# The opening of a two-block transformer kernel by half sections, and log counts added to the scores by TensorE

## The chip, the core and the metric

The kernel runs on one core of a Trainium2 chip. A core has TensorE (PE in the profile; PEld is its loading of weights), VectorE (DVE), ScalarE (ACT), GpSimd (POOL) and SyncE (SP), which here issues the loads. Each engine executes its own instructions in the order in which the program holds them; between engines there are only semaphores. The metric is the device time of one execution in microseconds (us), lower is better.

## The reference

Two blocks of two layers each, on 256 positions of width 1024, all in float32. What the change touches is the first block, in whose two layers `l` one finds:

```
mod = silu(c) @ w_mod[l] + b_mod[l]              # 1024 x 6144, one row
sh1, sc1, gt1, sh2, sc2, gt2 = split(mod, 6)
h = rms_norm(x, g) * (1 + sc1) + sh1
q_d, k_d, v_d, cq, ckv, k_rope = split(h @ w_in[l], ...)   # 1024 x 1952
# dilated heads (8 heads of 64), mixture of three window/dilation pairs
s = q.k * 64**-0.5 - slope_h * |distance|
...
# latent heads (8 heads): q = rms_norm(cq) @ w_q_up, its last 32 columns per head
# are normed and rotated: [x1*cos - x2*sin, x2*cos + x1*sin]
```

The mixture of the three dilated branches equals one softmax over all pairs of query and key whose scores have the logarithm of a count added: how many of the three branches see that pair. These log counts, 128 partitions x 512 for both tiles of queries, are a constant of the kernel and the same for all heads. Then follow the output product, an MLP, and the second block (stick-breaking and forgetting attention, a dense MLP and 8 experts), which the change does not touch.

## The kernel before

**Weights.** The kernel reads about 380 MB, nearly all of it float32 weights. SP loads them in pieces of 1 MB into a ring of six buffers, `raw`. A product in near float32 precision takes three passes of a rounded type (fp32r): ScalarE copies a piece rounded (`split`, L665, tile `w_high`), VectorE subtracts to get the remainder (`rest`, L1270, tile `w_low`), and TensorE multiplies high by high, high by low and low by high (`passes`, L2194). Activations are split in the same way (`h_high`, `h_low`). PE, ACT and DVE each hold such steps in an order that was written out by hand; `rest_to(w)` and `split_to(w)` mean all pieces up to `w`.

**Modulation.** Each section (l, s) of `mod` is computed from four pieces of `w_mod`, its quarters. The ones of the opening are (0,0) and (0,1), shift and scale of the first norm, and (0,2), the first gate. There a quarter is 256 columns by all 1024 rows: PE multiplies by a copy of silu(c) scaled by 1/32 (`c32`, in the profile c_columns_shared) into four strips of a bank (L2308, 16 matmuls), ACT copies the strips out (`store_rows`), PE adds them over the partitions with four tiny matmuls (`reduce_mod`, L2327), and DVE's `store_first(q)` adds the bias, 2 of the 8 blocks of 128 features at a time. Later sections are made in other ways, among them `BY_ROWS`: a quarter is 256 rows by all columns, 16 matmuls of 128x256 with 32 equal columns (L2301), read back by one transpose of 32x32 squares (L1407) and an add (L1409).

**The opening.** The first norm goes by blocks: DVE scales a block (`scaled_block`, L1351), ACT adds the shift and rounds (`h_high`, L756), DVE makes the remainder (`low_part`, L1340). It is done in four pairs, one per quarter, with the eight products of quarters between them. The pieces of `w_in` come in the order: columns from 1536 rows 0 to 511 (w0), the same columns rows 512 to 1023 (w1), then columns 0 to 511 (w2, w3) and 512 to 1023 (w4, w5) in two halves each. PE's `first_chunk` multiplies w0 against blocks 0 to 3, `second_chunk` w1 against blocks 4 to 7. Where PE has nothing to do, `turn_idly` (L2380) and `keep_busy` (L2268) issue matmuls whose results nobody reads. After w1 PE turns a stage of small vectors, which DVE's `store_vectors` (L1456, L1457) copies; then come w2, the positions (L2422 to L2424), w3, and the quarters of (0,2), their last two in front of the query up-projection (q_up).

**Latent and dilated stage.** When all of `w_in` is multiplied, PE does q_up (w6), kv_up (w7) and the rest of the w_in pieces (w8, w9), then the dilated heads, two at a time: `score_pair` (L2497, 8 matmuls), DVE's `max_head` (L1622) adds a bias to the scores and takes the maximum, ACT makes the exponentials, PE turns them (L2253) and multiplies by the values (L2539). The bias of a head is made by GpSimd: L628 scales the distances, L629 adds the log counts, into one of two tiles (dilated_bias, turned) that alternate, and a tile is free again when DVE has read it. DVE also rotates the latent queries between the heads (`mla_rotated`, L1605, and `mla_joined`, L1609 and L1610), and `mla_keys` (L1601) scales the latent keys. PE's `turn_mla` (L2564) needs both. In the first layer PE reduces section (0,2) (L2327, 16 matmuls) after the first `score_pair`, and DVE stores it (`store_mod(0, 2)`, L1409) after the first pair of maxima.

## Time and profile before

| | us |
|---|---|
| median of 3 runs | 1695.75 |
| lowest and highest | 1695.21, 1695.86 |
| the profiled execution, whole | 1694.58 |
| its span, first to last instruction | 1692.8 |
| its mean granted TensorE clock | 0.999 |
| PE busy in the span | 1656.1 |

A timeline row gives the start in us from the start of the span, the duration, engine, line and operation, out<-in by the program's names, and the shapes; "x16" says that 16 instructions stand in that row as one group, and the duration is then that of the group. In brackets stands the idle time of the engine just before, with what ended it. Matmuls are pipelined: the next one starts before the row of the last one ends, so the pace is read from the distance of two starts. Rows of the chain of waits follow the work back from the last instruction of the kernel, so they say whose lateness would move the end.

### The profile page before, as it was taken

To read this page: it belongs to the slowest core of one execution; us is meant where nothing else is said; L and a number is where in the kernel's file an instruction comes from. 1 tells how busy PE (TensorE), PEld (TensorE's weight loads), DVE (VectorE), ACT (ScalarE), POOL (GpSimd) and SP (SyncE) were. 2 spreads that over 40 slices of the span, in tenths; PEclk is the share of its full clock that TensorE was granted. 3 is DMA by queue.
4 is the path that set the end of the run, shared out by engine and by line. 5 is a ranking of instruction groups with operands and counts; after the bars stand their busy time and mean duration, and the time that the engine had idled before them with its cause. 6 is when DMAs were issued, how large, how long until landed. Compare 5 with 4: busy or idle time off the path is not lost.

```text
span 1692.8 us, 26664 instructions
## 1 busy us (share of the span) xinstructions
PE 1656.1 (98%) x10402; PEld 1422.0 (84%) x10402; DVE 1198.4 (71%) x1491; ACT 963.5 (57%) x1274; POOL 88.6 (5%) x105
## 2 busy tenths in 40 slices
PE   7999999999999999999999999999999999999998
PEld 5767898887688998898999999899888787887876
DVE  3775887777678555657585545557589888999887
ACT  4675534456754444546564434546567777667765
POOL 2050000003300000000000000000000000000000
PEclk9999999999999999999999999999999999999999
DMA  9765788845368655643256555553356999999995
GB/s 342 279 208 173 271 278 283 278 138 176 119 235 288 198 186 187 196 150 125 100 177 212 185 184 187 178 172 101 121 191 225 351 331 332 345 320 344 341 336 179
DMA packets 266362, 381.64 MB, mean 225 GB/s; under 512 B 8299, under 2 KB 201121, under 8 KB 266258
## 3 DMA queue, kind: packets, MB, share of 16 engines
q1 hardware_dynamic: 264592, 377.26, 66.8%
q0 software_dynamic: 1104, 1.76, 0.3%
q8 instruction: 72, 1.18, 0.3%
q10 hardware_dynamic: 562, 1.18, 0.2%
q14 instruction: 32, 0.26, 0.0%
HBM read 379.12 MB, written 1.05 MB: 225 GB/s over the span
## 4 chain that ended last, share of the span: by engine, by line
PE 83%; DVE 8%; ACT 4%; POOL 2%; issue 2%; DMA 1%; ACTq 0%; DVEq 0%
PE bank L2194 71%; DVE w_low L1270 4%; PE bank L2253 3%; ACT w_high L665 3%; PE bank L2509 1%; PE bank L2751 1%; DMA raw<-in_w_mod_dram 1%; PE bank L2539 1%; DVE mod_sums L1388 1%; PE bank L2301 1%; DMA x<-in_x_dram 1%; DVE turned L1351 1%; POOL dilated_bias L628 1%; POOL dilated_bias L629 1%; PE bank L2744 1%
## 5 line engine op out<-in xcount | busy, mean ns | idle before, releaser
L1270 DVE TENSOR_TENSOR w_low<-raw,w_high 128x2048 fp32r<-128x2048 f32 (+2 forms) x315 | 690.0, 2194 | 226.5 <-ACT w_high L665 225.0
L665 ACT ACTIVATE w_high<-raw 128x2048 fp32r<-128x2048 f32 (+3 forms) x333 | 596.4, 1797 | 219.3 <-PE bank L2194 211.0
L2194 PE MATMUL bank<-h_high,w_high 128*128 128x256 f32 x1200 | 342.8, 286 | 0.2
L2194 PE MATMUL bank<-h_high,w_low 128*128 128x256 f32 x1200 | 339.8, 283 | 0.0
L2194 PE MATMUL bank<-h_low,w_high 128*128 128x256 f32 x1200 | 339.8, 283 | 0.0
L2194 PE MATMUL bank<-w_high,h_high 128*128 128x512 f32 (+2 forms) x768 | 301.0, 392 | 8.5 <-DVE w_low L1270 7.5
L2194 PE MATMUL bank<-w_high,h_low 128*128 128x512 f32 (+2 forms) x768 | 292.1, 380 | 0.0
L2194 PE MATMUL bank<-w_low,h_high 128*128 128x512 f32 (+2 forms) x768 | 291.7, 380 | 0.0
L2194 PEld LDWEIGHTS bank<-h_high,w_high 128*128 128x128 f32 x1200 | 230.1, 192 | 5.3 <-issue 3.4
L2194 PEld LDWEIGHTS bank<-h_low,w_high 128*128 128x128 f32 x1200 | 230.1, 192 | 1.2
L2194 PEld LDWEIGHTS bank<-h_high,w_low 128*128 128x128 f32 x1200 | 230.0, 192 | 0.0
L2194 PE MATMUL bank<-w_high,act_high 128*128 128x512 f32 x544 | 213.7, 393 | 1.5 <-DVE act_low L1718 0.8
L2194 PE MATMUL bank<-w_low,act_high 128*128 128x512 f32 x544 | 211.7, 389 | 0.0
L2194 PE MATMUL bank<-w_high,act_low 128*128 128x512 f32 x544 | 211.3, 388 | 0.0
L2194 PEld LDWEIGHTS bank<-w_high,h_high 128*128 128x128 f32 x768 | 144.4, 188 | 45.0 <-DVE w_low L1270 14.2
L2194 PEld LDWEIGHTS bank<-w_high,h_low 128*128 128x128 f32 x768 | 144.4, 188 | 27.3
L2194 PEld LDWEIGHTS bank<-w_low,h_high 128*128 128x128 f32 x768 | 144.8, 189 | 24.1
L2194 PEld LDWEIGHTS bank<-w_high,act_high 128*128 128x128 f32 x544 | 102.3, 188 | 23.3 <-issue 1.3
L2194 PEld LDWEIGHTS bank<-w_high,act_low 128*128 128x128 f32 x544 | 102.1, 188 | 21.6
L2194 PEld LDWEIGHTS bank<-w_low,act_high 128*128 128x128 f32 x544 | 102.4, 188 | 18.8
L947 ACT ACTIVATE turned<-bank 128x512 f32<-128x512 f32 x32 | 19.1, 597 | 111.2 <-PE bank L2194 111.2
L1388 DVE SCALAR_TENSOR_TENSOR mod_sums<-raw,c_columns,mod_sums 128x512 f32<-128x512 f32 x70 | 52.6, 751 | 2.1
(355 smaller groups left out, 1822.4 us busy)
## 6 DMA issues: line engine op xcount, KB each, us to landing
raw<-in_w_gu_exp_dram SPq DMA_DIRECT2D x160, 512.0 KB, 5.4
raw<-in_w_in_dram SPq DMA_DIRECT2D x52, 1024.0 KB, 5.3
raw<-in_w_mod_dram SPq DMA_DIRECT2D x48, 1024.0 KB, 5.9
raw<-in_w_dn_exp_dram SPq DMA_DIRECT2D x40, 1024.0 KB, 6.4
raw<-in_w_mlp_in_dram SPq DMA_DIRECT2D x32, 1024.0 KB, 5.9
raw<-in_w_mlp_out_dram SPq DMA_DIRECT2D x32, 1024.0 KB, 5.2
raw<-in_w_gu_dense_dram SPq DMA_DIRECT2D x22, 1024.0 KB, 5.1
raw<-in_w_out_dram SPq DMA_DIRECT2D x16, 1024.0 KB, 5.1
```

The costliest lines, as they stand in the source:

```text
L628: step(nc.gpsimd.tensor_scalar(dst[:, :], dist[:, :], -(2.0 ** -(h + 1)), None, ALU.mult))
L629: nc.gpsimd.tensor_tensor(dst[:, :], dst[:, :], con[:, C_LNM:C_LNM + TT * S], ALU.add).then_inc(bias_ready, 1)
L665: return nc.scalar.activation(dst, src, ACT.Copy, scale=scale)
L947: nc.scalar.activation(relu[:, 0, slot, :], psum[slot][:, :], ACT.Relu).then_inc(f_one[l], 1)
L1270: V.tensor_tensor(wlo[w % SPLIT][:, 0:n], raw[raw_of(w) % RAW][:, 0:n], whi[w % SPLIT][:, 0:n].bitcast(F32), ALU.subtract).then_inc(raw_us ...
L1351: V.scalar_tensor_tensor(f, turned_bank(n, k), scale(k), rs_row, ALU.mult, ALU.mult).then_inc(h_float, 1)
L1388: ins = V.scalar_tensor_tensor(acc, vk, ccol[:, k:k + 1], acc, ALU.mult, ALU.add)
L2194: ins = T.matmul(out, lhsT, rhs, start=start and i == 0, stop=stop and i == len(pairs) - 1)
L2253: return T.transpose(out, src, ident)
L2301: ins = T.matmul(mod_strips_of(l, s)[32 * g:32 * g + 32, :], ccol[:, 2 * q + k:2 * q + k + 1].to_broadcast([P, 32]), rows[:, g, :, :], sta ...
L2509: ins = T.matmul(psum[e][:, S * t:S * t + S], qT[:, m, P * t:P * t + P], kT[:, m, :], start=True, stop=True)
L2539: ins = T.matmul(psum[4][DH * e:DH * e + DH, 0:S], v, pturn[:, e, S * kt:S * kt + S], start=kt == 0, stop=kt == TT - 1, skip_group_check=True)
```

## The change

It has three parts.

**Opening.** A quarter of (0,0) and (0,1) is now 512 columns by 512 rows, and its 16 matmuls are 128x128 with the unscaled `ccol`. They go straight into strips in bank 6 (first half of the features) or bank 0 (second half), so ACT's `store_rows` and PE's `reduce_mod` are gone for these sections; `store_first(half)` waits for four products, transposes, adds and scales for both sections, and is followed by four blocks of the norm instead of two. (0,2) becomes a section by rows: it has no `store_rows` or reduction either, `store_mod(0, 2)` moves from after the first maxima to ahead of `rest_to(w + 6)`, and PE waits for it ahead of q_up instead of ahead of the value product. The pieces of `w_in` come in another order, in both layers: w0 (columns from 1536) and w1 (columns 0 to 511) with rows 0 to 511, then w2 and w3 the same with rows 512 to 1023. PE multiplies all of w0 and w1 between the first half's products and the second half's, where blocks 4 to 7 were made beside w0 before.

**Log counts.** GpSimd splits the log counts once per layer (three instructions), PE adds them to the scores by eight more matmuls per pair of heads, and GpSimd's L629 is gone for all heads.

**Queries.** The six instructions of the rotation go from DVE to GpSimd, between the biases of heads 3 and 4; `mla_keys` moves ahead by a pair, and DVE waits for the rotation ahead of `store_mod(l, 3)`.

```diff
-    after = {(0, 0): [-1, -1, 0, 1], (0, 1): [-1, -1, 0, 1], (0, 2): [2, 3, 4, 5]}
+    after = {(0, 0): [-1, -1, 1, 1], (0, 1): [-1, -1, 1, 2], (0, 2): [3, 4, 5, 5]}
...
-BY_ROWS = ((0, 3), (0, 4), (1, 3), (1, 4))
+BY_ROWS = ((0, 2), (0, 3), (0, 4), (1, 3), (1, 4))
...
         def first_norm():
...
+            def high(blocks):
+                high_blocks(0, blocks, lambda k: modc[:, 0, k:k + 1])
             norm_squares(0)
-            store_rows(0, 1, 0)
-            store_rows(0, 0, 1)
             store_rs(0)
...
+            high(range(2))
             split_to(0)
...
+            high(range(2, 4))
+            split_to(2)
+            high(range(4, KD))
...
+        def store_first(half):
+
+            dve.wait_ge(mod_product, 4 * half + 4)
+            c = slice(4 * half, 4 * half + 4)
+            step(V.transpose(mod_turned, first_strips(half)))
+            columns = mod_turned.rearrange("p (s k i) -> p s k i", s=2, i=32)[:, :, :, 0]
+            biases = vec[:, V_BM:V_BM + 16].rearrange("p (s k) -> p s k", s=2)
+            step(V.tensor_tensor(modc[:, 0:2, c], columns, biases[:, :, c], ALU.add))
+            step(V.scalar_tensor_tensor(modc[:, 1, c], modc[:, 1, c], 1.0, vec[:, V_G1 + 4 * half:V_G1 + 4 * half + 4], ALU.add, ALU.mult))
+            V.sem_inc(mod_stored, 1)
...
+            for half in range(2):
+                store_first(half)
+                if half == 0:
                     dve.wait_ge(rs_out, 1)
+                for k in range(4 * half, 4 * half + 4):
                     scaled_block(0, k, scale_of)
+                    if k % 4:
+                        low_part(0, k - 1, shift_of)
+                low_part(0, 4 * half + 3, shift_of)
+                if half == 0:
+                    rest_to(2)
...
             if l == 0:
                 store_vectors()
-            rest_to(w + 3)
+            rest_to(w + 4)
...
             V.tensor_tensor(latlo, latent, lathi.bitcast(F32), ALU.subtract).then_inc(lat_low, 1)
+            if l == 0:
+                store_mod(0, 2)
             rest_to(w + 6)
...
+        multiply_first(0, 1)
         spread_rs(0)
...
+        turn_idly(2)
+        multiply_first(1, 0)
+        turn_idly(2)
+        multiply_first(1, 1)
+        turn_idly(2)
+        keep_busy(4, 5, 0)
...
+        natural(0, 0, W0, [psum[4 + t] for t in range(TT)], True, False, 0)
+        multiply_first(0, 2)
+        natural(1, 0, 512, [psum[6 + t] for t in range(TT)], True, False, None, [0])
+        multiply_first(0, 3)
+        natural(1, 0, 512, [psum[6 + t] for t in range(TT)], True, False, None, [1])
+        multiply_first(1, 2)
+        turn_idly(4, 1)
+        multiply_first(1, 3)
+        turn_idly(4, 1)
+        later_chunk(4, W0, 2)
...
+            if l == 0:
+                pe.wait_ge(mod_stored, stored_of(0, 2))
             pe.wait_ge(proj_out, 4 * l + 2)
...
+                pe.wait_ge(counts_ready, l + 1)
+                for e in range(2):
+                    for t in range(TT):
+                        for i, counts in enumerate((counts_high, counts_low)):
+                            ins = T.matmul(psum[e][:, S * t:S * t + S], ident_high, counts[:, S * t:S * t + S],
+                                           start=False, stop=i == 1, skip_group_check=True)
+                    ins.then_inc(head_scored, 1)
...
-                step(nc.gpsimd.tensor_scalar(dst[:, :], dist[:, :], -(2.0 ** -(h + 1)), None, ALU.mult))
-                nc.gpsimd.tensor_tensor(dst[:, :], dst[:, :], con[:, C_LNM:C_LNM + TT * S], ALU.add).then_inc(bias_ready, 1)
+                nc.gpsimd.tensor_scalar(dst[:, :], dist[:, :], -(2.0 ** -(h + 1)), None, ALU.mult).then_inc(bias_ready, 1)
```

What stands in a row on TensorE around the last two quarters of the opening. Before (banks 4 and 5 take the columns from 1536, 128x416 an instruction; L2308 is a quarter, L2327 its reduction, L2268 idle matmuls):

```order
L2194 MATMUL bank5<-w_high,h_low 128x416
L2327 MATMUL bank7<-ones,mod_sums 128x1 x2
L2308 MATMUL bank6<-raw2,c_columns_shared 32x256 x8
L2268 MATMUL bank1<-w_high 128x512 x2
L2327 MATMUL bank7<-ones,mod_sums 128x1 x2
L2268 MATMUL bank1<-w_high 128x512 x3
L2308 MATMUL bank0<-raw3,c_columns_shared 32x256 x8
L2194 MATMUL bank4<-w_high,h_high 128x416
```

The last quarter (bank 0) came after w0, the 24 matmuls of 128x416 into banks 4 and 5. Now, from the end of w1 on, which fills banks 6 and 7 (L2276 is a quarter, L2331 idle matmuls, L2162 the passes):

```order
L2162 MATMUL bank7<-w_high,h_high 128x512
L2162 MATMUL bank7<-w_low,h_high 128x512
L2162 MATMUL bank7<-w_high,h_low 128x512
L2276 MATMUL bank0<-raw2,c_columns 32x128 x16
L2331 MATMUL bank1<-x,constants 128x256 x4
L2276 MATMUL bank0<-raw4,c_columns 32x128 x16
L2331 MATMUL bank1<-x,constants 128x256 x4
L2162 MATMUL bank4<-w_high,h_high 128x416
```

The last quarter of the opening (from buffer 4) now stands behind 24 matmuls of 128x416 and 24 of 128x512.

On VectorE, behind the last remainder of the first norm, before (L1270 is `rest`, L1456 and L1457 `store_vectors`):

```order
L1340 SCALAR_TENSOR_TENSOR h_low<-turned,mod_columns,h_high 128x256 [waits h_high_ready] x2
L1270 TENSOR_TENSOR w_low<-raw,w_high 128x2048 [waits weights_high_done]
L1456 COPY vector_columns<-bank 128x128 [waits setup_tensor]
L1457 CAST rope_products<-dilated_bias 1x256
L1270 TENSOR_TENSOR w_low<-raw,w_high 128x2048 [waits weights_high_done,setup_vector]
```

And now (L1324 is the remainder of a block, L1437 and L1438 `store_vectors`, L1254 `rest`):

```order
L1324 SCALAR_TENSOR_TENSOR h_low<-turned,mod_columns,h_high 128x256 [waits h_high_ready] x2
L1437 COPY vector_columns<-bank 128x128 [waits setup_tensor]
L1438 CAST rope_products<-dilated_bias 1x256
L1254 TENSOR_TENSOR w_low<-raw,w_high 128x2048 [waits weights_high_done,setup_vector]
L1254 TENSOR_TENSOR w_low<-raw,w_high 128x2048 [waits weights_high_done]
```

The wait for the turned stage now stands ahead of both `rest` steps, those of w3 and w4. Further on in the same engine, ahead of q_up's piece, before:

```order
L1558 TENSOR_TENSOR act_low<-turned,act_high 128x768 [waits latent_high]
L1270 TENSOR_TENSOR w_low<-raw,w_high 128x1536 [waits weights_high_done]
L1307 TENSOR_TENSOR statistics<-statistics 128x16 [waits rsqrt_guess_ready]
```

And now, with `store_mod(0, 2)` (L1388, L1390) between:

```order
L1539 TENSOR_TENSOR act_low<-turned,act_high 128x768 [waits latent_high]
L1388 STREAM_TRANSPOSE rope_products<-bank 128x256 [waits mod_quarter_multiplied]
L1390 TENSOR_TENSOR mod_columns<-rope_products,vector_columns 128x8 [waits vector_step]
L1254 TENSOR_TENSOR w_low<-raw,w_high 128x1536 [waits vector_step,weights_high_done]
```

The remainder of q_up's piece now stands behind the wait for the last quarter of (0,2).

## Rows read from the trace of the kernel before

The columns of a timeline row are told above.

**Rows 1.** The page: busy time, and the chain that ended last, by engine.

```profile
PE 1656.1 (98%) x10402; PEld 1422.0 (84%) x10402; DVE 1198.4 (71%) x1491; ACT 963.5 (57%) x1274; POOL 88.6 (5%) x105
...
PE 83%; DVE 8%; ACT 4%; POOL 2%; issue 2%; DMA 1%; ACTq 0%; DVEq 0%
```

**Rows 2.** A window: busy PE, PEld, DVE, ACT, POOL; clock, DMA share, GB/s.

```profile
20.00:30.00 10.00, 9.47 (x82) 6.53 (x82) 5.50 (x12) 4.42 (x8) 0.00 (x0) 1.00 1.09 362
```

**Rows 3.** Chain of waits, the opening: start, us, engine, output, line.

```profile
45.37 5.74 PE bank L2194 x24
...
59.11 0.81 PE bank L2253 x6
```

**Rows 4.** Timeline of PE, the opening.

```profile
17.65 0.41 PE L2253 MATMUL bank<-constants,statistics 128*128 128x128 f32 x2
...
22.26 1.11 PE L2380 MATMUL bank<-x,constants 128*128 128x256 f32 x4
...
25.62 0.46 PE L2194 MATMUL bank<-w_high,h_high 128*128 128x416 f32 x1
...
28.00 0.50 PE L2327 MATMUL bank<-ones,mod_sums 128*128 128x1 f32 x4
...
36.52 1.07 PE L2308 MATMUL bank<-raw,c_columns_shared 128*32 128x256 f32 x16
```

**Rows 5.** Timeline of DVE, the opening.

```profile
22.90 0.88 DVE L1351 SCALAR_TENSOR_TENSOR turned<-bank,mod_columns,reciprocal_sums_spread 128x256 f32<-128x256 f32 x2
...
23.69 1.88 DVE L1270 TENSOR_TENSOR w_low<-raw,w_high 128x1664 fp32r<-128x1664 f32 x1
...
45.23 0.28 DVE L1456 COPY vector_columns<-bank 128x128 f32<-128x128 f32 x1
...
46.89 2.29 DVE L1270 TENSOR_TENSOR w_low<-raw,w_high 128x2048 fp32r<-128x2048 f32 x1 [1.18 <-ACT w_high L665]
```

**Rows 6.** Timeline of ACT, the opening.

```profile
21.58 1.58 ACT L665 ACTIVATE w_high<-raw 128x1664 fp32r<-128x1664 f32 x1
```

**Rows 7.** Timeline of PE, q_up and dilated heads of the first layer.

```profile
73.85 0.50 PE L2194 MATMUL bank<-w_high,act_high 128*128 128x512 f32 x1
...
75.57 0.28 PE L2194 MATMUL bank<-w_high,act_low 128*128 128x256 f32 x1
...
94.88 1.84 PE L2327 MATMUL bank<-ones,mod_sums 128*128 128x1 f32 x16
...
97.65 1.13 PE L2497 MATMUL bank<-turned 64*128 64x256 f32 x8
...
113.38 1.07 PE L2301 MATMUL bank<-raw,c_columns 128*32 128x256 f32 x16
```

**Rows 8.** Timeline of DVE, the remainder of the piece of q_up.

```profile
69.73 1.76 DVE L1270 TENSOR_TENSOR w_low<-raw,w_high 128x1536 fp32r<-128x1536 f32 x1 [2.84 <-ACT w_high L665]
```

**Rows 9.** Timeline of GpSimd, dilated heads of the first layer.

```profile
95.69 1.49 POOL L628 TENSOR_SCALAR dilated_bias<-distance 128x512 f32<-128x512 f32 x1 [0.96 <-DVE negative_max L1622]
```

**Rows 10.** Groups of GpSimd, second layer: count, busy us, mean ns, idle before.

```profile
L629 POOL TENSOR_TENSOR turned<-turned,constants 128x512 f32<-128x512 f32 x4 | 5.1, 1280 | 0.3
...
L602 POOL TENSOR_TENSOR natural<-natural,trig 128x32 f32<-128x32 f32 x4 | 4.9, 1248 | 0.1
```

**Rows 11.** Timeline of PE, the second layer.

```profile
351.86 0.43 PE L2319 MATMUL bank<-mod_sums,ones 128*32 128x128 f32 x8
...
375.73 0.50 PE L2194 MATMUL bank<-w_high,h_high 128*128 128x512 f32 x1 [0.49 <-DVE w_low L1270]
...
417.00 1.14 PE L2497 MATMUL bank<-turned 64*128 64x256 f32 x8 [0.29 <-ACT turned L665]
...
436.47 1.07 PE L2301 MATMUL bank<-raw,c_columns 128*32 128x256 f32 x16
```

**Rows 12.** Timeline of DVE, a section that is stored through the transpose.

```profile
352.35 0.45 DVE L1407 STREAM_TRANSPOSE rope_products<-bank 128x256 f32<-128x256 f32 x1 [1.25 <-PE bank L2319]
```

**Rows 13.** Timeline of PE, the 16 transposes of the first norm.

```profile
11.96 3.42 PE L2253 MATMUL bank<-constants,x 128*128 128x128 f32 x16 [2.07 <-DMA x<-in_x_dram]
```

291 lines of the change are left out of this document (94 added, 197 removed).

## The prediction

> **What bounds the kernel now.** I read the page first: TensorE is busy for 98% of the span, and 83% of the chain that ended last runs over it [rows 1]. A stall of PE, or work added to it, so counts one for one unless it falls into a wait that PE has already. Then came the window, timelines and chain of the opening. There the loads run at 362 GB/s [rows 2], a piece of 1.05 MB every 2.9 us, and PE works between them: first matmul of w0 at 25.62, last quarter of the first two sections at 36.52 [rows 4], w2 from 45.37, and the first quarter of (0,2) at 58.1, 1.0 ahead of the transposes at 59.11 [rows 3]. Last came the heads. There GpSimd hands out a bias per head in two steps of about 1.5 and 1.3 [rows 9, 10], and DVE, and behind it PE, wait for it.
>
> **A quarter.** 16 instructions of 128 columns take the place of 8 of 256 (two trace records each). The same columns would take 1.0 as now [rows 4]; four times the 0.36 between the starts of the 8 short records at 351.86 and what follows would be 1.44 [rows 11]. I take 1.2, nearer to the first, since the same data pass.
>
> **Opening, first half.** PE's spreading of the norm's roots ends at 17.95, as before (17.65 plus its pace of 0.3) [rows 4]. Then stand two idle matmuls (0.42 each, by 1.11 for four records with the tail taken off [rows 4]), a quarter, two idle ones and the fourth quarter: 17.95 + 0.84 + 1.2 + 0.84 + 1.2 = 22.0. The tiny reductions and ACT's copies, which cost PE about 0.5 each here [rows 4], are gone, but nothing of the norm can start earlier than this. `store_first` is a transpose of 0.45 and two small steps [rows 12], 1.0 in all: 23.05. Four blocks take DVE 0.40 for each of two operations (two in 0.79 before the next starts) [rows 5], 3.2; ACT has w0's rounding of 1.58 [rows 6] between blocks 1 and 2, and DVE waits for that, so the last remainder ends at 27.4. w0's remainder, 1.88 [rows 5], stands behind all four blocks now, where before it started at 23.69. So w0's product starts at **29.3 instead of 25.6**.
>
> **Opening, PE up to the last quarter.** w0 is 24 matmuls at the pace of 12 in 2.3 (25.62 to 28.00) [rows 4], 4.6. w1 is 24 of 512 columns, 5.7 [rows 3]. Between them stand four quarters, 4.8, and four idle matmuls, 1.7: 29.3 + 4.6 + 5.7 + 4.8 + 1.7 = 46.1. The last quarter's load isn't late: one more piece stands ahead of it than before, so it is there at 36.5 + 2.9 = 39.4 [rows 2, 4]. The second norm half starts only now: store 1.0, then DVE and ACT in turn at 0.8 a block, remainders at 48.3 to 50.7. w2's first four steps follow them and the rest, 2.3, stands behind: 53.7. PE waits for about 3.0 in this, partly under idle matmuls.
>
> **Opening, the stage.** DVE then waits for PE's transpose of the stage, which PE does after w2 (54.0), stores the vectors, 0.5 (0.28 and one alike) [rows 5], and only then makes w3's remainder, 2.29 [rows 5]: 56.8. Queued behind that wait are the remainders of w3 and w4, and PE has nothing else: it stands for **2.9**. Put the other way round, w3's remainder would have been ready at 53. w3's product and the positions take 5.7 and 1.3: 63.8. Before, the same point came at 58.0. **Sum of the opening: +5.8**; with quarters of 1.0 or 1.44, +5.0 or +6.8.
>
> **Ahead of q_up.** From there PE has three quarters' and two pieces' work, with the same transposes: 15.9 as between 58.1 and 73.85 [rows 3, 7]: 79.7. Then it needs DVE's `store_mod(0, 2)`, 1.0 as above, and the remainder of q_up's piece, 1.76 [rows 8], which is queued behind it on DVE now. Before, that remainder was ready 2.3 ahead of PE. **+2.8**. Should DVE's other work be late by then, this grows; it can't fall under 1.0.
>
> **To the second pair of heads.** The 16 reductions after the first scores go, −1.84 [rows 7]. The counts come: 8 fp32r matmuls of 256 columns per pair of heads, at the 0.12 between two such starts [rows 7], 0.94 a pair, 1.88 for two. DVE's and ACT's places shift by some tenths: **+0.35**.
>
> **Dilated heads, first layer.** From the end of the second scores (97.65 + 1.07) to the end of the product at 113.38 [rows 7] it is 15.7 now, the pace of GpSimd's four steps per pair. With one step per head GpSimd is no bound; PE's own work per pair is: scores 2.0, turning 0.9, a quarter 1.0, values and spreading 1.45, together 5.35. That gives 13.9, **−1.8**. The rotation, six GpSimd steps of 256 elements, is bounded by half of the 1.28 for 512 elements and by the 1.25 that 32 elements took beside a busy DVE [rows 10]; I take 0.7, nearer to the first, since those 1.25 were a rare case. Then it hides beside PE up to 1.0 each.
>
> **Second layer.** The new order of pieces lets two products follow without the waits for remainders, such as the 0.49 at 375.73 [rows 11]: −0.7, of which I give back 0.3 for GpSimd's three counts steps beside DVE: **−0.4** (0 to −0.7). Its heads take 20.5 from 417.0 to the end of the product at 436.47 [rows 11]; two more pieces are multiplied among them, PE has little slack, and the 0.94 a pair takes what GpSimd gives: **−0.1** (−0.5 to +1.2).
>
> **The sum**: 5.8 + 2.8 + 0.35 − 1.8 − 0.4 − 0.1 = +6.65. On the profiled execution's 1694.58 that is 1701.2; the median stands 1.17 above that execution, so **1702.4**.
>
> **Rivals.**
> *The clock falls.* The 16 transposes at 11.96 took 3.42 [rows 13], 0.21 each, right after PE had been idle; the six at 59.11 took 0.81, 0.135 each [rows 3], though the granted clock reads 1.00 in the window of the opening [rows 2]. That is what 1.2 GHz instead of 2.4 would look like. PE has little between 22.0 and 29.3 now: idle matmuls of 0.84, then a wait, four idle ones, a wait. If w0's product starts so, it loses between half of 3.4 and all of it, and the time is 1704.1 to 1705.8, say 1705. For: these waits are the longest of the opening. Against: before, PE was thinly busy here too. The Trainium skill ("TensorE: Matmul & The Clock Gate", "Part 1: The HAM clock gate (the "warmup" mystery)") says that the array's default is the halved clock and that activity releases it. By that rule this rival is the rule's own result, and the trace's first transposes agree with it. Chance 0.15.
>
> *The opening stays bound by loads.* The last quarter is multiplied when it arrives, at 39.4 instead of 44.9, and 5.5 of the sum go: 1696.9, no measurable change. It decides if w0's product starts by 23.8. For: before, PE waited for loads here. Against: the order of DVE's queue, by which w0's remainder can't start before the fourth block. Chance 0.10.
>
> *Faster.* The same, and the counts' matmuls of three pairs in each layer vanish in waits of PE for ACT, 2 x 2.8: 1691.3. Against it speaks that PE's own work fills a pair. Chance 0.07.
>
> *GpSimd is slow at the rotation.* From 1.0 a step it delays the biases of heads 4 and 5 and `turn_mla`; at 1.25 it costs 6 x 0.25 per layer, 3.0 in all (1705.4), at 1.5 about 6 (1708.4). For: DVE works beside it all the time. The Trainium skill ("SBUF — State Buffer", the entry "shared port pair") has the two engines share a pair of ports that one holds for a whole instruction while the other blocks fully. That agrees with the group of mean 1248 ns, and by it the price would be the upper one. Chance 0.07.
>
> **How the numbers follow.** The forecast, 0.61, holds from 1699 to 1705 by the bounds of the terms (quarters −0.8 to +1.0, second layer to +1.6, DVE's order ±1). About what a measurement can tell from no change is 0.2%, 3.4 us: up to 1692.3 is faster, from 1699.2 slower. Faster 0.07; same 0.10 and the forecast's lower edge, 0.05: 0.15; slower 0.78. The range from 1696.0 to 1706.5 takes in the load rival and the clock rival and leaves out the faster one, most of GpSimd's and a tail of 0.06.
>
> **What would show it.** In the profile after: w0's first matmul near 29.3; the last quarter of the opening near 45, not 39; PE idle by about 3 ahead of w3's product with DVE's remainder as its end, and about 2.8 ahead of q_up with `store_mod` and the remainder behind it; score to score 5.35 in the first layer's heads; six GpSimd steps near 0.7; second layer's w5 ended 0.7 earlier after its start. The forecast is wrong if the two waits ahead of w3 and q_up aren't there, or if w0 starts before 26.

## The result and the profile after

| | before | changed kernel |
|---|---|---|
| median | 1695.65 us (4 runs) | 1707.68 us (4 runs, 1707.00 to 1708.16) |
| the profiled execution, whole | 1694.58 | 1707.88 |
| its span | 1692.8 | 1706.1 |
| its mean granted clock | 0.999 | 0.995 |
| forecast | | 1702.4, range 1696.0 to 1706.5 |

The change makes the kernel slower by 0.7%: the ratio to the kernel before is 1.0071, 95% interval 1.0054 to 1.0088. The sign was forecast, the size was not: +12.0 us where +6.65 was worked out, and 1.2 us outside the range. The page's row of busy time is the first thing to hold against [rows 1]:

```profile
PE 1666.3 (98%) x10563; PEld 1434.1 (84%) x10563; DVE 1186.0 (70%) x1474; ACT 959.1 (56%) x1261; POOL 78.8 (5%) x107
```

PE has 161 more matmul records (the counts, more idle ones, the shorter quarters, less the reductions), and its busy time grows by 10.2 us. A part of that is the same work done more slowly, and the windows say where. The columns are the stretch, its length, busy time of PE, PEld, DVE, ACT and POOL, the granted clock, the DMA share and GB/s:

```profile
20.00:30.00 10.00, 5.91 (x68) 3.76 (x57) 6.21 (x13) 4.98 (x6) 0.00 (x0) 0.81 1.05 386
...
30.00:40.00 10.00, 10.00 (x72) 8.61 (x76) 3.90 (x2) 1.60 (x1) 0.00 (x0) 0.85 0.93 330
...
60.00:70.00 10.00, 10.00 (x51) 7.26 (x50) 5.51 (x23) 3.50 (x4) 0.00 (x0) 0.83 0.33 110
...
80.00:90.00 10.00, 7.23 (x54) 5.24 (x53) 6.69 (x12) 5.23 (x7) 0.00 (x0) 0.88 0.90 332
```

Before, each of these stretches had a granted clock of 1.00, as [rows 2] has for the first. Now all four are below it (and 90 to 100 reads 0.95), in three places: 26 to 33, 60 to 64 and 87 to 91 us. Cut finer, the clock reads 0.50 or just above it in them, so this is 1.2 GHz in place of 2.4.

The timeline of PE says what stands ahead of each of the three (columns as in [rows 4]):

```profile
26.74 2.07 PE L2236 MATMUL bank<-w_high 128*128 128x512 f32 x4 [3.05 <-ACT w_high L675]
...
29.86 0.71 PE L2162 MATMUL bank<-w_high,h_high 128*128 128x416 f32 x1 [1.05 <-DVE w_low L1254]
...
31.06 0.55 PE L2162 MATMUL bank<-w_high,h_high 128*128 128x416 f32 x1
...
33.24 0.35 PE L2162 MATMUL bank<-w_low,h_high 128*128 128x416 f32 x1
...
46.80 1.08 PE L2276 MATMUL bank<-raw,c_columns 128*32 128x128 f32 x32
...
58.91 0.50 PE L2162 MATMUL bank<-w_high,h_high 128*128 128x512 f32 x1 [2.90 <-DVE w_low L1254]
...
60.95 0.63 PE L2162 MATMUL bank<-w_low,h_high 128*128 128x512 f32 x1
...
86.16 0.47 PE L2162 MATMUL bank<-w_high,act_high 128*128 128x512 f32 x1 [2.77 <-DVE w_low L1254]
...
89.38 0.63 PE L2162 MATMUL bank<-w_low,act_high 128*128 128x512 f32 x1
```

The first row is the four idle matmuls after a wait of 3.05 us; then w0's product starts at 29.86 after 1.05 more. Its matmuls of 416 columns have a duration of 0.55 and a pace of 0.35 (31.06) where they later have 0.35 and 0.19 (33.24). w3's product starts at 58.91 after 2.90, full at first, then at 0.63 a matmul instead of 0.39. q_up starts at 86.16 after 2.77, and the same happens from 87.5 on. In the chain of waits the first product is a single row that answers to the row of 24 matmuls in [rows 3]:

```profile
29.86 6.19 PE bank L2162 x24
```

Twenty-four matmuls of 416 columns take 6.1 us, against 4.6 at full rate. w3's take 7.3 (58.91 to 66.20) against 5.7, and q_up with kv_up 8.6 (86.16 to 94.73) against 7.05. The three stretches cost 1.5, 1.6 and 1.5: **4.6 us**.

The waits themselves are the forecast ones. DVE's timeline shows why PE stood there:

```profile
56.05 0.29 DVE L1437 COPY vector_columns<-bank 128x128 f32<-128x128 f32 x1 [3.32 <-PE bank L2363]
...
56.56 4.49 DVE L1254 TENSOR_TENSOR w_low<-raw,w_high 128x2048 fp32r<-128x2048 f32 x2
...
83.46 0.45 DVE L1388 STREAM_TRANSPOSE rope_products<-bank 128x256 f32<-128x256 f32 x1 [2.95 <-PE bank L2269]
...
84.25 1.76 DVE L1254 TENSOR_TENSOR w_low<-raw,w_high 128x1536 fp32r<-128x1536 f32 x1
```

DVE waits 3.32 for PE's transposed stage (L1437), then makes two remainders in a row (L1254), and PE's w3 needs the first. DVE waits 2.95 for PE's last quarter of (0,2) (L1388), stores it, and only then makes q_up's remainder. In both places each engine waits for the other in turn.

| Point in the program (PE) | before | forecast | after |
|---|---|---|---|
| first matmul of w0 | 25.6 | 29.3 | 29.9 |
| last quarter of the opening | 36.5 | 44.9 | 46.8 |
| w3's product starts | 52.3 | 56.8 | 58.9 |
| w3's product and the positions done | 58.0 | 63.8 | 67.5 |
| q_up starts | 73.85 | 82.5 | 86.2 |
| second pair of scores done | 98.7 | 107.75 | 112.9 |
| quarter behind `turn_mla` done | 114.4 | 121.65 | 126.9 |
| first scores of the second layer | 417.0 | | 429.0 |
| quarter behind `turn_mla` there, start | 436.5 | | 448.6 |

Read down the last column minus the first: +4.3, +10.3, +6.6, +9.5, +12.3, +14.2, +12.5, +12.0, +12.1. (The product of w3 stands ahead of the positions now and behind them before, so +6.6 is not on the same footing.) All is lost by 113 us; the first layer's heads give back 1.7 and the second layer's projections 0.7. From 448.6 us to the last matmul the distance moves only from 12.1 to 11.5 (it starts at 1686.07 before and at 1697.59 after). The two profiled executions are 13.3 apart, since in the slower one the last results took 1.8 longer to be stored behind that matmul; the medians are 12.0 apart.

### The profile page after: what moved, and what is told of

It reads as the page before. It is cut to its first block, busy times and chain, and to the rows that moved or that the text cites. A ratio compares the mean times of both kernels' runs of the same rounds, so it can differ in the third digit from the quotient of the medians.

```text
span 1706.1 us, 26932 instructions
## 1 busy us (share of the span) xinstructions
PE 1666.3 (98%) x10563; PEld 1434.1 (84%) x10563; DVE 1186.0 (70%) x1474; ACT 959.1 (56%) x1261; POOL 78.8 (5%) x107
## 3 DMA queue, kind: packets, MB, share of 16 engines
HBM read 379.12 MB, written 1.05 MB: 223 GB/s over the span
## 4 chain that ended last, share of the span: by engine, by line
PE 86%; DVE 7%; ACT 4%; issue 1%; DMA 1%; ACTq 0%; DVEq 0%
PE bank L2162 73%; DVE w_low L1254 4%; PE bank L2221 3%; ACT w_high L675 3%; PE bank L2269 1%; PE bank L2486 1%; PE bank L2458 1%; PE bank L2696 1%; DVE mod_sums L1372 1%; DMA x<-in_x_dram 1%; PE bank L2689 0%; PE bank L2726 0%; PE bank L2729 0%; PE bank L2447 0%; PE bank L2441 0%
## 5 line engine op out<-in xcount | busy, mean ns | idle before, releaser
L1254 DVE TENSOR_TENSOR w_low<-raw,w_high 128x2048 fp32r<-128x2048 f32 (+2 forms) x315 | 689.4, 2192 | 223.2 <-ACT w_high L675 221.4
L2162 PE MATMUL bank<-h_high,w_high 128*128 128x256 f32 x1200 | 342.4, 285 | 0.2
L2162 PE MATMUL bank<-h_low,w_high 128*128 128x256 f32 x1200 | 339.5, 283 | 0.0
L2162 PE MATMUL bank<-h_high,w_low 128*128 128x256 f32 x1200 | 339.4, 283 | 0.0
L2162 PE MATMUL bank<-w_high,h_high 128*128 128x512 f32 (+2 forms) x768 | 301.9, 393 | 11.0 <-DVE w_low L1254 9.7
L2162 PE MATMUL bank<-w_high,h_low 128*128 128x512 f32 (+2 forms) x768 | 292.8, 381 | 0.0
L2162 PE MATMUL bank<-w_low,h_high 128*128 128x512 f32 (+2 forms) x768 | 292.6, 381 | 0.0
L2162 PEld LDWEIGHTS bank<-h_high,w_high 128*128 128x128 f32 x1200 | 230.0, 192 | 5.3 <-issue 3.4
L2162 PEld LDWEIGHTS bank<-h_low,w_high 128*128 128x128 f32 x1200 | 230.0, 192 | 1.2
L2162 PEld LDWEIGHTS bank<-h_high,w_low 128*128 128x128 f32 x1200 | 229.9, 192 | 0.0
L2162 PE MATMUL bank<-w_high,act_high 128*128 128x512 f32 x544 | 214.4, 394 | 4.3 <-DVE w_low L1254 2.8
L2162 PE MATMUL bank<-w_low,act_high 128*128 128x512 f32 x544 | 212.1, 390 | 0.0
L2162 PE MATMUL bank<-w_high,act_low 128*128 128x512 f32 x544 | 211.7, 389 | 0.0
L2162 PEld LDWEIGHTS bank<-w_high,h_high 128*128 128x128 f32 x768 | 145.2, 189 | 46.7 <-DVE w_low L1254 16.6
L2162 PEld LDWEIGHTS bank<-w_high,h_low 128*128 128x128 f32 x768 | 145.1, 189 | 27.7
L2162 PEld LDWEIGHTS bank<-w_low,h_high 128*128 128x128 f32 x768 | 145.6, 190 | 24.2
L2162 PEld LDWEIGHTS bank<-w_high,act_high 128*128 128x128 f32 x544 | 102.7, 189 | 26.5 <-issue 4.3
L2162 PEld LDWEIGHTS bank<-w_high,act_low 128*128 128x128 f32 x544 | 102.7, 189 | 21.7
L2162 PEld LDWEIGHTS bank<-w_low,act_high 128*128 128x128 f32 x544 | 102.9, 189 | 18.7
```

The costliest lines, as they stand in the source:

```text
L1254: V.tensor_tensor(wlo[w % SPLIT][:, 0:n], raw[raw_of(w) % RAW][:, 0:n], whi[w % SPLIT][:, 0:n].bitcast(F32), ALU.subtract).then_inc(raw_us ...
L2162: ins = T.matmul(out, lhsT, rhs, start=start and i == 0, stop=stop and i == len(pairs) - 1)
```

## The experiments

Two theories ran through the first four. **A wait costs itself and the clock behind it**: each wait of about 3 us is followed by some 3 us of matmuls at half rate, which adds 1.5. **Waits only**: the slow matmuls have another cause, for example the loads that run beside them. All ratios are against runs of the kernel before that stood beside each kernel on its chip; the changed kernel itself was not timed again, so its 1707.7 is taken from the first runs. The medians of the kernel before in these groups of runs lie from 1695.65 to 1697.55, so a difference between medians of two groups is uncertain by 1 to 2.

### One order of DVE at a time

```diff
 # a_vectors
+            rest_to(w + 3)
             if l == 0:
                 store_vectors()
             rest_to(w + 4)
 # a_store_mod
+            rest_to(w + 6)
             if l == 0:
                 store_mod(0, 2)
-            rest_to(w + 6)
```

> The changed kernel with one thing undone: DVE makes w3's remainder before it waits for the turned stage of small vectors, as the kernel before did; everything else as changed. Theory (a wait costs itself and the clock behind it): the wait of 2.9 us ahead of w3's product shrinks to under 0.5, and the half-rate matmuls that follow it (nine of w3's product at 0.43 us instead of 0.23) are gone, another 1.6: 1707.7 falls by 4.0 to 4.5, to about 1703.4. The granted clock between 60 and 64 us reads 1.00 instead of 0.56. Rival (waits only, the slow matmuls have another cause, such as the loads that run beside them): the time falls by 2.5 to 2.9, to 1705, and w3's product keeps its slow stretch.

Measured: 1703.57 us, ratio 1.0041 (1.0027 to 1.0055). That is 4.1 less, as the theory of the clock has it; the rival had 1705. PE's timeline of this kernel:

```profile
56.99 0.50 PE L2163 MATMUL bank<-w_high,h_high 128*128 128x512 f32 x1 [0.39 <-DVE w_low L1254]
...
82.62 0.47 PE L2163 MATMUL bank<-w_high,act_high 128*128 128x512 f32 x1 [2.77 <-DVE w_low L1254]
```
```profile
60.00:70.00 10.00, 10.00 (x59) 1.00 0.49 183
...
80.00:90.00 10.00, 7.38 (x38) 1.00 1.00 370
```

The wait ahead of w3 is 0.39 now, and the clock behind it is at 1.00. The second row is a lesson of its own: the wait ahead of q_up is still 2.77, and yet, in this execution, the clock doesn't fall behind it. A wait of that length brings the fall in some executions and not in others; the runs of this kernel lie between 1703.07 and 1705.38.

> The changed kernel with one thing moved: DVE makes the remainder of q_up's piece before it stores section (0,2), instead of after. Theory (a wait costs itself and the clock behind it): PE still waits for the store ahead of q_up, but 1.0 us instead of 2.8, and such a short wait leaves the clock at full: -1.8 for the wait and -1.7 for the twelve or so matmuls at half rate at 88 to 91 us, together 3.3 to 3.7, to about 1704.2. Rival (waits only): -1.8, to 1705.9.

Measured: 1704.78 us, ratio 1.0045 (1.0029 to 1.0061), with runs from 1703.22 to 1706.93. The gain is 2.9, nearer to the theory's 3.5 than to the rival's 1.8, but the spread of its runs takes in both. Its profile is the slowest of them:

```profile
34.35 0.55 PE L2162 MATMUL bank<-w_high,h_high 128*128 128x416 f32 x1
...
60.17 0.80 PE L2162 MATMUL bank<-w_high,h_high 128*128 128x512 f32 x1 [2.90 <-DVE w_low L1254]
...
86.69 0.47 PE L2162 MATMUL bank<-w_high,act_high 128*128 128x512 f32 x1 [0.88 <-issue]
```
```profile
80.00:90.00 10.00, 9.12 (x67) 1.00 0.88 323
```

The wait ahead of q_up is 0.88 and the clock behind it is full. What makes this execution slow is the other two falls. In the first, at 34.35, w0's matmuls are still at 0.55, where in the changed kernel's profile they were fast from 33.0 on. From w0's product to the first matmul of w2 it takes 21.9 here and 20.8 there. The second fall is longer too: the clock reads 0.50 already when w3's product starts at 60.17, and the product takes 8.4 (to 68.61) against 7.3 in the changed kernel and 5.7 at full rate. So the same fall costs more in one execution than in another, here 2.5 and 2.7 in place of 1.5 and 1.6.

### Idle matmuls in the waits, and nothing else

```diff
-        turn_idly(2)
-        keep_busy(4, 5, 0)
+        turn_idly(8)
+        keep_busy(12, 5, 0)
...
+            if l == 0:
+                turn_idly(6, 1)
             natural(w + 3, 4, 512, [psum[6 + t] for t in range(TT)], False, True)
...
             if l == 0:
+                turn_idly(5, 1)
                 pe.wait_ge(mod_stored, stored_of(0, 2))
```

> The changed kernel with idle matmuls, whose results nobody reads, put into PE's three long waits (ahead of w0, of w3 and of q_up); no wait, order or result is changed, so each wait keeps its end. Theory (clock): PE doesn't fall to half rate behind them, which gives back 1.5, 1.6 and 1.7 us: -4.8, to about 1702.9, with a mean granted clock of 0.999 instead of 0.995. Rival (waits only): nothing is given back, 1707.7, or somewhat more, if the last idle matmul of a wait ends after the wait would have.

Measured: 1703.50 us, ratio 1.0041 (1.0027 to 1.0056), mean granted clock 0.999. This is the sharpest of the runs, since no order and no result is touched and 4.2 us are gone (4.8 were expected). Its slowest run, 1704.82, is below the fastest of the changed kernel, 1707.00, and in the profile its last matmul starts 3.9 earlier. From w2's first matmul to w3's it takes 8.28 as before the edit, so that wait of DVE's is untouched; from w3's to q_up it takes 25.67 instead of 27.25, the 1.6 of the second fall:

```profile
49.65 0.43 PE L2162 MATMUL bank<-w_high,h_high 128*128 128x416 f32 x1 [0.83 <-DVE h_low L1324]
...
57.93 0.50 PE L2162 MATMUL bank<-w_high,h_high 128*128 128x512 f32 x1 [0.31 <-DVE w_low L1254]
...
83.60 0.47 PE L2162 MATMUL bank<-w_high,act_high 128*128 128x512 f32 x1 [0.41 <-DVE w_low L1254]
```

w0's product starts at 30.25 and w2's first matmul follows at 49.65, 19.4 later; in the changed kernel it was 20.8, in the run above 21.9. That prices the first fall alone: 1.4 and 2.5; in the profiles of the runs with one and with both orders, further above and below, it is 1.8 (21.2) and 2.0 (21.4). The loads beside it moved at 386 GB/s from 20 to 30 us in both kernels, so they are not what made the matmuls slow.

### Both orders, and then the first wait filled

> Both orders of DVE's work at once: w3's remainder ahead of the wait for the stage, q_up's remainder ahead of the store of (0,2). Theory (a wait costs itself and the clock behind it): the two gains add, 4.2 + 3.5, to about 1700.0; what is left above the kernel before is the late start of w0 with its clock and the late second half of the norm. Rival (waits only): 2.7 + 1.8, to 1703.2. Rival (absorbed: PE waits later for ACT or DVE work that is no earlier): less than either single gain adds up to, 1702 or more, with new waits behind w3 or q_up.

Measured: 1700.85 us, ratio 1.0026 (1.0016 to 1.0036), 6.8 less than the changed kernel: 4.1 and 2.9 add. The third theory, that the work is merely late elsewhere, falls.

```profile
57.23 0.50 PE L2163 MATMUL bank<-w_high,h_high 128*128 128x512 f32 x1 [0.38 <-DVE w_low L1254]
...
80.96 0.47 PE L2163 MATMUL bank<-w_high,act_high 128*128 128x512 f32 x1 [0.88 <-issue]
```

These answer to 58.91 and 86.16. What is left ahead of q_up is a wait of 0.88 for the store.

> The changed kernel with both orders of DVE's work as in the run that had both, and idle matmuls in the one wait that is still long, ahead of w0. Theory (a wait costs itself and the clock behind it): w0's product still starts near 30, but at full rate, which gives back 1.3 to 2.3 of 1700.9, to about 1699.2; what then is left above the kernel before is the late start of w0 and of the norm's second half, less 1.0 for the heads and the second layer. Rival (waits only): 1700.9, no change.

Measured: 1699.70 us, ratio 1.0015 (1.0006 to 1.0025). 1.15 less than without the idle matmuls, a little under the range of 1.3 to 2.3 (by the two ratios it is 1.9), and both kernels' runs overlap (1699.05 to 1701.52 against 1699.95 to 1701.79). In its profile w0's product starts at 29.84 and q_up at 78.73, 2.2 ahead of the run without them, and so it stays until 1272 us. Then 1.4 of it is lost in the second block, which the edit doesn't touch:

```profile
1275.70 2.05 PE L2991 MATMUL bank<-picks,h_rows_high 128*128 128x256 f32 x8 [0.84 <-DVE picks L2001]
```

The same eight records take 1.19 in the run without the idle matmuls, and the granted clock from 1276 to 1278 reads 0.50 here, behind a wait of 0.84 only. So this is one more fall of the clock. In which of the other runs it came can't be told, but the six runs up to 1699.72 have a mean clock of 0.999 and the four from 1700.54 on have 0.998.

### The start of w0's product

What was left above the kernel before is w0's late start. Between the orders of the changed kernel and a new opening stands one run. It has both orders of DVE's work too, and against the run before it two things are changed: w0 is rounded and its remainder made earlier, and the idle matmuls between the first quarters are gone, which then stand ahead of w0. The edit, against the changed kernel, without the two orders shown above:

```diff
-            high(range(2))
             split_to(0)
-            high(range(2, 4))
+            high(range(4))
             split_to(2)
...
                 for k in range(4 * half, 4 * half + 4):
                     scaled_block(0, k, scale_of)
+                    if k == 1:
+                        rest_to(0)
...
-        turn_idly(2)
         multiply_first(1, 0)
-        turn_idly(2)
         multiply_first(1, 1)
-        turn_idly(2)
-        keep_busy(4, 5, 0)
+        turn_idly(4)
+        keep_busy(8, 5, 0)
```

> Between the run with both orders of DVE's work and the run with the new opening: the loads and PE's products in the order of the changed kernel, but w0 is rounded ahead of the norm's blocks, its remainder made after the second block, and the idle matmuls of the opening stand in the wait ahead of w0. Theory (the order within the first half is most of the loss): w0's product starts near 24.7 at full rate, the last quarter near 41.5 instead of 46.8, q_up near 73.5; 5.2 below the run with both orders and the filled wait (1699.7), so 1694.5, and the order of the loads and quarters is worth the other 2.8 of the new opening. Rival (the quarters' place behind w0 and w1 is most of the loss, since DVE or the loads are the bound behind it): 1697 or more.

Measured: 1694.63 us, ratio 0.9989 (0.9980 to 0.9998), 5.1 below the run before it (4.4 by the ratios). The profiled executions are 5.9 apart: 4.5 are there at q_up, and about 1.5 more come near 1276 us, where this one has no fall. ACT had been idle for 5.2 us ahead of the norm's blocks in the changed kernel, and w0 is there in that time: ACT rounds it from 19.60 on, and is idle again before the first block. Rounding it there costs nothing.

```profile
24.89 0.43 PE L2164 MATMUL bank<-w_high,h_high 128*128 128x416 f32 x1 [0.59 <-DVE h_low L1323]
...
40.92 1.08 PE L2278 MATMUL bank<-raw,c_columns 128*32 128x128 f32 x32
...
74.26 0.47 PE L2164 MATMUL bank<-w_high,act_high 128*128 128x512 f32 x1 [0.88 <-issue]
```

w0 starts at 24.89 instead of 29.84, and q_up at 74.26 instead of 78.73. Of the 5.0 at w0, 2.1 are the idle matmuls between the quarters: the last of the first four quarters ends at 20.5 instead of 22.5, and DVE's store starts at 20.60 instead of 22.67. The other 2.9 are w0's place in the orders of ACT and DVE. Now q_up stands 0.4 behind the kernel before, and the later gains of the change, in the heads and the second layer, make up for it.

The new opening goes further. All quarters of the second half are loaded behind w0, one of them behind w1, and PE multiplies them as they come, ahead of w1:

```diff
-    after = {(0, 0): [-1, -1, 1, 1], (0, 1): [-1, -1, 1, 2], (0, 2): [3, 4, 5, 5]}
+    after = {(0, 0): [-1, -1, 0, 0], (0, 1): [-1, -1, 0, 1], (0, 2): [3, 4, 5, 5]}
...
+        natural(0, 0, W0, [psum[4 + t] for t in range(TT)], True, False, 0, [0])
+        multiply_first(0, 2)
+        natural(0, 0, W0, [psum[4 + t] for t in range(TT)], True, False, None, [1])
+        multiply_first(0, 3)
+        multiply_first(1, 2)
+        turn_idly(3, 1)
+        multiply_first(1, 3)
+        turn_idly(2, 1)
+        natural(1, 0, 512, [psum[6 + t] for t in range(TT)], True, False)
...
+            for t in (range(TT) if l else (1, 0)):
+                if l == t == 0:
+                    pe.wait_ge(mod_stored, stored_of(0, 2))
```

> The changed kernel with another opening by halves. Both orders of DVE's work from the earlier pair of runs; all quarters of the second half are loaded behind w0, the last of them behind w1, and multiplied right after w0; ACT rounds w0 before the norm's blocks, DVE makes its remainder after the second block; half 2 of the norm stands behind w1's remainder; idle matmuls fill the waits; q_up begins with the banks that the store of (0,2) doesn't read. Theory (what is wrong with the opening is its order, not the halves): w0's product starts near 24.8 instead of 29.9 and at full clock, the last quarter is multiplied near 35 instead of 46.8, q_up starts near 70 instead of 86; the whole takes about 1691, below both kernels. Rival (halves are at fault: the second half can't be normed before its last quarter, which loads too late for PE to have enough to do): q_up starts at 75 or later and the time stays at 1695 or above.

Measured: 1691.68 us, ratio 0.9966 (0.9952 to 0.9979). This version is faster than the kernel before by 0.34%, and than the changed one by 1.0% (0.9966 over 1.0071).

```profile
24.57 0.43 PE L2165 MATMUL bank<-w_high,h_high 128*128 128x416 f32 x1 [0.60 <-DVE h_low L1325]
...
34.34 1.08 PE L2279 MATMUL bank<-raw,c_columns 128*32 128x128 f32 x32
...
42.87 0.46 PE L2165 MATMUL bank<-w_high,h_high 128*128 128x416 f32 x1 [0.91 <-DVE w_low L1255]
```

w0 starts at 24.57 (expected 24.8), the last quarter at 34.34 (35), w2 at 42.87 where the changed kernel had 50.63, and q_up right behind the last quarter of (0,2), near 70.3 (70). So sections by halves are not at fault; their place in the orders of four engines was.

Without the idle matmuls:

> The kernel with the new opening, but without the idle matmuls in its waits (22 to 24.5, 33 to 34.3 and 35.4 to 36.5 us). Theory (a wait costs itself and the clock behind it): the first wait, 4 us long without them, brings half rate for the start of w0, +1.5 to +2.3 on 1691.7: 1693.6, with the clock of 20 to 30 us below 0.9. Rival (the order alone does it, idle matmuls don't matter here): 1691.7 within 0.5.

Measured: 1692.32 us (1690.77 to 1694.17), ratio 0.9971 (0.9961 to 0.9981). That is 0.6 above the kernel with them, between the rival's 0.5 and the theory's 1.5 to 2.3, and the intervals of the two ratios overlap: no loss that can be told, though the fall came:

```profile
24.44 0.43 PE L2165 MATMUL bank<-w_high,h_high 128*128 128x416 f32 x1 [4.36 <-DVE h_low L1325]
...
26.15 0.55 PE L2165 MATMUL bank<-w_high,h_high 128*128 128x416 f32 x1
...
34.26 1.08 PE L2279 MATMUL bank<-raw,c_columns 128*32 128x128 f32 x32 [0.28 <-DMA raw<-in_w_mod_dram]
```
```profile
20.00:30.00 10.00, 5.64 (x50) 0.83 1.05 387
```

The wait ahead of w0 is 4.36, the clock of 20 to 30 us reads 0.83, and w0's first half runs at 0.55 a matmul. But the last quarter starts at 34.26 after waiting 0.28 for its load, against 34.34 above, and w2 starts at 42.81 against 42.87. PE had time to spare ahead of that load, so the slow matmuls ended no later than the load did. **A slow clock costs only where PE is what ends last**, which neither of the two expectations had. One profiled execution shows it here; in others the fall may last longer, and the eight other runs have mean clocks from 0.996 to 0.999.

### The heads

The heads' part alone, put into the kernel before (its core):

```diff
-                step(nc.gpsimd.tensor_scalar(dst[:, :], dist[:, :], -(2.0 ** -(h + 1)), None, ALU.mult))
-                nc.gpsimd.tensor_tensor(dst[:, :], dst[:, :], con[:, C_LNM:C_LNM + TT * S], ALU.add).then_inc(bias_ready, 1)
+                nc.gpsimd.tensor_scalar(dst[:, :], dist[:, :], -(2.0 ** -(h + 1)), None, ALU.mult).then_inc(bias_ready, 1)
...
+                for e in range(2):
+                    for t in range(TT):
+                        for i, counts in enumerate((counts_high, counts_low)):
+                            ins = T.matmul(psum[e][:, S * t:S * t + S], ident_high, counts[:, S * t:S * t + S],
+                                           start=False, stop=i == 1, skip_group_check=True)
```

> The kernel before with only the part on the heads: log counts added by PE's eight matmuls per pair, GpSimd scales only and rotates the latent queries; opening, order of pieces and section (0,2) stay as before. Theory (PE's own work is what it trades): in the first layer the two first pairs' matmuls cost 1.9 and the shorter pairs behind them give back 1.3 to 1.8, in the second layer 0.2 is lost; together +0.3 to +0.8: 1696.2. Rival (GpSimd was the bound and its relief is a gain): -1.8 in the first layer and none lost in the second, 1694. Rival (GpSimd and DVE hold each other up over the rotation): +2 or more.

Measured: 1696.65 us beside 1697.55 for the kernel before, ratio 1.0000 (0.9990 to 1.0009): no change that can be told. The interval, -1.7 to +1.5 us, takes in the theory's +0.3 to +0.8, leaves the first rival's -1.8 just outside and shuts out the second; the trace is sharper, below. And the reverse, the old heads in the new opening:

> The same kernel, but with the heads as in the kernel before: GpSimd adds the log counts, DVE rotates the latent queries. Theory (PE's own work is what it trades): 0.3 to 0.8 below the run with the new heads, about 1690.4. Rival (GpSimd's relief is a gain): 1.5 to 3 above it.

Measured: 1693.14 us (10 runs), 1.5 above the new heads (5 runs). **Here the expectation was wrong in sign**, though the runs of the two overlap (1691.39 to 1694.15 against 1690.41 to 1693.06), so the profiles have to say it. From the first dilated scores to the first latent ones the first layer takes 23.5 in the kernel before (92.3 to 115.8) and 23.75 with the new heads put into it (95.6 to 119.3), and the second layer 21.9 and 22.1, so the relief of GpSimd is no gain there. In the new opening the first layer takes 23.3 with the old heads and 22.2 with the new:

```profile
90.39 1.13 PE L2439 MATMUL bank<-turned 64*128 64x256 f32 x8
...
106.95 1.13 PE L2439 MATMUL bank<-turned 64*128 64x256 f32 x8 [0.98 <-DVE negative_max L1592]
...
110.25 0.64 PE L2504 MATMUL bank<-constants,turned 128*96 128x128 f32 x4 [1.14 <-DVE turned L1580]
...
113.71 1.99 PE L2451 MATMUL bank<-gate_rows,mla_q_turned 96*128 96x256 f32 x8
```
```profile
90.23 1.13 PE L2442 MATMUL bank<-turned 64*128 64x256 f32 x8
...
112.45 1.99 PE L2459 MATMUL bank<-gate_rows,mla_q_turned 96*128 96x256 f32 x8
```

With the old heads PE waits for DVE's maximum, which is behind GpSimd's bias, 0.98, and for the rotation, 1.14; all its waits in this stage make 4.5, against 3.35 in the kernel before. With the new heads it has none. Taking only the reductions away gains 0.2 of their 1.8 (23.5 to 23.3), since the rest comes back as waits for GpSimd; taking only GpSimd's work away gains nothing (23.75), since PE's own work fills the stage; both together gain 1.3. My terms of -1.84 and -1.8 were right only as a pair. Of the 1.5 between the two medians the first layer's heads are 1.1; the second layer's give back 0.25; the rest is not placed.

### The spread of the kernel before

> The kernel before with two more idle matmuls in its opening, behind the spreading of the roots and behind the third quarter, where PE is thinly busy. Its own runs spread from 1695 to 1700 and the run with its opening and the other heads had matmuls at half rate from 21.8 to 28.5 us. Theory (that spread is the clock in the opening): fewer runs fall, and the median comes to the lower end, 1695.5, with a spread of under 2. Rival (the spread has another cause): median and spread as those of the kernel before beside it; or the two idle matmuls delay the quarters by up to 1 us and it is slower by that.

Measured: 1697.26 us (1695.02 to 1698.90), ratio 1.0002 (0.9993 to 1.0011). The rival holds: nothing gained. In this kernel's profile w0's product starts at 27.12 instead of 25.62. Of these 1.5 us, 1.05 are there ahead of the idle matmuls (the roots are spread at 18.70 instead of 17.65), behind a first quarter that took 1.93 where it had taken 1.07:

```profile
15.80 1.93 PE L2308 MATMUL bank<-raw,c_columns_shared 128*32 128x256 f32 x16
```

So the idle matmuls delayed w0 by at most 0.45. The granted clock reads 1.00 beside this quarter, though its pace is half that of the later ones; in the first 18 us a reading of 1.00 proves little. That the opening of the kernel before falls now and then is shown by one trace, that of the run with its opening and the new heads, which took 1699.81:

```profile
19.62 1.07 PE L2316 MATMUL bank<-raw,c_columns_shared 128*32 128x256 f32 x16
...
21.80 1.81 PE L2316 MATMUL bank<-raw,c_columns_shared 128*32 128x256 f32 x16
...
27.25 1.81 PE L2316 MATMUL bank<-raw,c_columns_shared 128*32 128x256 f32 x16
```

The same 16 records of a quarter take 1.07, then 1.81 twice; the granted clock reads 0.50 from 22 to 28 us. The longest wait of PE behind 17 us and ahead of the fall was 0.60. The spread of the kernel before, from 1694.7 to 1700.8, goes with the clock: each run has a mean granted clock on record, and of the 77 that stood beside the other kernels the five above 1700 read 0.995 to 0.997, the 23 below 1696 read 0.998 or 0.999. Where in those runs it fell only a profile could tell. None of the eleven runs with more idle matmuls is above 1698.9, against three of the 26 beside them above 1700, which is too few to say that they keep the worst falls away.

## Why the prediction was right or wrong

**Quarters.** The taken value of 1.2 was too high: 32 records have a pace of 1.0 (46.80 to 47.81), the lower bound. It gave back 0.8 in the four quarters behind w0's start.

**First half of the opening.** Forecast 29.3 for w0, measured 29.86. The order of DVE's queue was the cause, as worked out. 0.6 comes from `x`, which landed at 12.5 where it had landed at 11.9 before; the run with the old opening and the new heads had that too (12.59), and the one with two more idle matmuls had 12.00, so it differs between executions.

**Up to the last quarter, and the stage.** The last quarter came at 46.8 instead of 44.9: 0.6 from w0's late start, 1.5 from the clock and 0.25 from four idle matmuls, which take 1.93 (44.87 to 46.80) instead of 1.7, less 0.6 for three quarters; 0.15 is left. Waits of 0.83 in front of w2 and 2.90 in front of w3 were measured; 2.9 was forecast for the second, with its place and its end. 2.77 in front of q_up answers to 2.8. The step that counted instructions behind a moved wait held to 0.1 us.

**The clock: the step that failed.** The sum priced all new waits at themselves and had no term for matmuls at half rate behind them. The clock was named only as a rival, with a chance of 0.15, for one place, at 1.7 to 3.4. It came at all three waits of about 3 us, 4.6 together in the profiled execution: with it the sum is 1707.0, and 1707.6 with the late `x`. Two things were wrong in it. The evidence against, that PE had been thinly busy in the opening before without falling, came from one execution, in which the longest wait between 15 and 59 us was 1.3; the three new waits are twice that, and all four runs of the changed kernel read 0.995. And the opening before does fall in some executions: the trace with that opening and the new heads has it, behind waits of 0.50 and 0.60. And once I had written down two waits of 2.8 and 2.9, I priced each at itself, although the rival's own reason applied to them as much as to the first. The Trainium skill ("TensorE: Matmul & The Clock Gate", "Part 1: The HAM clock gate (the "warmup" mystery)") has exactly the halved clock as the default and activity as what lifts it; the trace agrees, with 0.50 as the granted clock behind each wait.

**To the second pair, and the heads.** +0.35 was forecast, +0.3 came behind q_up's slow stretch (18.1 against 17.8 from the transposes behind q_up on). The first layer's heads gave -1.7 against -1.8. GpSimd's rotation:

```profile
112.32 1.44 POOL L607 TENSOR_TENSOR rope_products<-turned 128x256 f32<-128x256 f32 x2
...
113.72 1.42 POOL L607 TENSOR_TENSOR natural<-turned 128x256 f32<-128x256 f32 x2
...
115.22 1.59 POOL L609 TENSOR_TENSOR turned<-rope_products 128x256 f32<-128x256 f32 x1
...
116.78 0.72 POOL L610 TENSOR_TENSOR turned<-natural 128x256 f32<-128x256 f32 x1
```

Five of its six steps of 256 elements take 0.7, as taken, and the subtraction 1.59, 5.2 in all in place of 4.2. PE shows no wait for it, so that rival didn't come true. From score to score it takes 5.5 to 5.7 (110.75, 116.43, 121.97), where 5.35 was counted.

**Second layer.** Projections -0.7 (forecast -0.4, with 0.3 given back for GpSimd that wasn't needed), heads +0.2 (-0.1):

```profile
428.97 1.14 PE L2441 MATMUL bank<-turned 64*128 64x256 f32 x8
...
448.60 1.07 PE L2269 MATMUL bank<-raw,c_columns 128*32 128x256 f32 x16
```

**The other rivals.** The opening didn't stay bound by loads: the last quarter was multiplied at 46.8, not at 39.4. That rival named a lever that is there, w0's start: the run that brings it to 24.9, together with both orders of DVE's work, has q_up only 0.4 behind the kernel before, though its last quarter is still multiplied only at 40.9. The faster one didn't come.

**The range** left 1707.7 out because the clock's price stood in it once. Slower, at 0.78, came true.

## What to carry to other kernels

Where an edit adds a wait of nearly 3 us ahead of a dense stretch of TensorE, add the price of the clock behind it, here 1.4 to 2.7 for each, unless TensorE has time to spare there before its next load; idle matmuls in the wait take that price away at little cost (w0's product started at 30.25 instead of 29.86, and 0.16 of that was `x`). Don't take one profile with a full clock as proof that a stage keeps it: look at the mean clock of all runs. When an instruction that waits for TensorE is moved up in another engine's queue, look at what it now stands in front of: two such moves cost 4.1 and 2.9 us here. When a step hides another engine's delay, taking away either alone gains next to nothing.

## What the runs showed of the hardware

The same wait, 2.77 us ahead of q_up, was followed by half rate in one kernel's execution and by full rate in another's, and a fall ahead of w0 lasted until 33.0 in one and until 35.4 in another. So a kernel with waits near this length has a wide spread of times (1703.2 to 1706.9 for one of them), and one profile doesn't give its price. Long waits aren't the only occasion: in the second block the clock fell behind a wait of 0.84 in two of the thirteen profiled executions, near 1276 and near 1268 us, and in the first of them it cost 1.4. Loads whose rows are 512 columns moved at 386 GB/s from 20 to 30 us in the changed kernel, against 362 in the kernel before, whose quarters there are 256 columns wide [rows 2]; I had counted 2.9 us a piece for both.
